# Seven-product pairs at two places of a feed-forward stage, their blocks loaded from another queue

## The reference

```python
def swiglu(x, w_in, w_out):
    gate, up = jnp.split(x @ w_in, 2, axis=-1)
    return (jax.nn.silu(gate) * up) @ w_out

# first block, i = 0, 1
x = x + 0.5 * swiglu(rms_norm(x, ffn1_norm_g[i]), ffn1_w_in[i], ffn1_w_out[i])   # ffn0, ffn2
x = x + concat(mixer_heads, memory_heads) @ w_out
x = x + 0.5 * swiglu(rms_norm(x, ffn2_norm_g[i]), ffn2_w_in[i], ffn2_w_out[i])   # ffn1, ffn3
# second block
h = h + hybrid_mixer(rmsnorm(h, norm_mix_w), ...)
h = h + (silu(n @ w_gate) * (n @ w_up)) @ w_down      # n = rmsnorm(h, norm_ffn_w): ffn4
return rmsnorm(h, final_norm_w)
```

## Time and profile before

| what | us |
|---|---|
| median of 3 runs | 1527.47 (1527.09 to 1528.89) |
| the profiled execution | 1527.58 |
| its span in the trace | 1525.9 |
| PE busy | 1515.7 |
| DVE busy | 1110.0 |
| ACT busy | 867.3 |
| POOL busy | 263.8 |

### The profile page before, as it was taken

How to read it: one execution, slowest core, us unless ns; L and a number is a source line. 1 busy time by engine, 2 the same in 40 slices (tenths; PEclk the granted TensorE clock), 3 DMA queues, 4 the chain that set the end, 5 groups by cost and what they waited for, 6 DMA issues and landing times.

```text
span 1525.9 us, 19569 instructions
## 1 busy us (share of the span) xinstructions
PE 1515.7 (99%) x7714; PEld 1281.9 (84%) x7714; DVE 1110.0 (73%) x1211; ACT 867.3 (57%) x1087; POOL 263.8 (17%) x216
## 2 busy tenths in 40 slices
PE   9999999999999999999999999999999999999998
PEld 7888888888888888888888888899988888888886
DVE  6687766556787568776776788599998568667875
ACT  7545554646455554556776455476887344454554
POOL 0222200001132122220001232100571000012220
PEclk9999999999999999999999999999999999999999
DMA  7997656446976699765416975666554665579762
GB/s 253 308 262 222 188 173 200 138 166 217 276 219 195 182 289 259 217 188 179 151 56 213 305 226 185 207 190 203 180 182 145 215 193 188 174 219 302 211 185 101
DMA packets 274307, 311.40 MB, mean 204 GB/s; under 512 B 64272, under 2 KB 233512, under 8 KB 274216
## 3 DMA queue, kind: packets, MB, share of 16 engines
q1 hardware_dynamic: 273112, 308.84, 65.4%
q10 hardware_dynamic: 1104, 1.31, 0.3%
HBM read 295.92 MB, written 1.09 MB: 195 GB/s over the span
## 4 chain that ended last, share of the span: by engine, by line
PE 94%; issue 2%; DVE 2%; ACT 1%; POOL 1%; DMA 1%; ACTq 0%; DVEq 0%; POOLq 0%
PE ps L2371 24%; PE ps L2375 24%; PE ps L2372 24%; PE ps L2413 3%; PE ps L2587 2%; PE ps L2588 2%; PE ps L2586 2%; PE ps L2361 2%; PE ps L2363 2%; PE ps L2362 2%; PE ps L2414 1%; PE ps L2429 1%; PE ps L2542 1%; DMA scr<-in_mem_dram 1%; PE ps L2693 0%
## 5 line engine op out<-in xcount | busy, mean ns | idle before, releaser
L1411 DVE TENSOR_TENSOR w_lo<-w_raw,w_hi 128x2048 fp32r<-128x2048 f32 x250 | 592.0, 2372 | 175.4 <-ACT w_hi L793 175.1
L793 ACT ACTIVATE w_hi<-w_raw 128x2048 fp32r<-128x2048 f32 x250 | 477.1, 1912 | 229.0 <-PE ps L2375 210.0
L2371 PE MATMUL ps<-w_hi,xg 128*128 128x512 f32 (+1 forms) x960 | 375.0, 391 | 0.0
L2375 PE MATMUL ps<-w_hi,xg 128*128 128x512 f32 (+1 forms) x960 | 372.1, 388 | 0.0
L2372 PE MATMUL ps<-w_lo,xg 128*128 128x512 f32 (+1 forms) x960 | 372.0, 387 | 0.0
L2371 PE MATMUL ps<-w_hi,y_hi 128*128 128x512 f32 x666 | 261.6, 393 | 0.5 <-DVE w_lo L1418 0.2
L2375 PE MATMUL ps<-w_hi,y_lo 128*128 128x512 f32 x666 | 259.1, 389 | 0.0
L2372 PE MATMUL ps<-w_lo,y_hi 128*128 128x512 f32 x666 | 258.9, 389 | 0.0
L761 POOL COPY scr<-scr 128x512 uint16<-128x512 uint16 x100 | 112.8, 1144 | 778.9 <-DVE scr L1526 778.9
L2371 PEld LDWEIGHTS ps<-w_hi,xg 128*128 128x128 f32 x960 | 180.3, 188 | 37.2 <-issue 0.7
L2375 PEld LDWEIGHTS ps<-w_hi,xg 128*128 128x128 f32 x960 | 180.2, 188 | 37.0
(11 more groups left out here) (409 smaller groups left out, 1864.1 us busy)
## 6 DMA issues: line engine op xcount, KB each, us to landing
w_raw<-in_ffn_w_in_dram SPq DMA_DIRECT2D x168, 512.0 KB, 4.9
w_raw<-in_ffn_w_out_dram SPq DMA_DIRECT2D x88, 512.0 KB, 4.8
w_raw<-in_w_in_dram SPq DMA_DIRECT2D x82, 512.0 KB, 4.5
w_raw<-in_a_w_in_dram SPq DMA_DIRECT2D x28, 512.0 KB, 4.6
w_raw<-in_w_down_dram SPq DMA_DIRECT2D x22, 512.0 KB, 4.5
w_raw<-in_w_gate_dram SPq DMA_DIRECT2D x21, 512.0 KB, 4.0
w_raw<-in_w_up_dram SPq DMA_DIRECT2D x21, 512.0 KB, 5.0
y_raw<-in_ffn_w_in_dram SPq DMA_DIRECT2D x16, 512.0 KB, 5.4
```

The lines of the kernel that those rows point to most:

```text
L793: act.activation(w_hi[:, u % RING, :], w_raw[:, u % RING, :], ACT.Copy).then_inc(w_rounded, 1)
L1411: dve.tensor_tensor(w_lo[:, s, :], w_raw[:, s, :], w_hi[:, s, :].bitcast(F32), ALU.subtract).then_inc(w_split, 1)
L2371: pe.matmul(dst, xh, hi, start=start, stop=False, skip_group_check=True)
L2375: return pe.matmul(dst, xl, hi, start=False, stop=stop, skip_group_check=True)
```

## The change

`PAIRS_OF` gives the pieces at which a pair begins, for each stage: 8 in ffn0 and ffn1, 4 and 8 in ffn2, ffn3 and ffn4, where before it was 7 in all five. Places of units come from `ffn_places`. SP no longer loads blocks. POOL does, at places between its cuts and joins; for a stage's second pair each block waits for the product of the first pair that reads the same buffer. The T and S work of DVE and ACT moves to the two or three steps ahead of the first pair, and that of a second pair to the end of the first and to step 7. The S sums and their parts are made once a stage and serve both pairs. A pair at 8 takes in the last piece, with its transposition on PE.

```diff
-PAIR = 7
-
-
-def gate_at(i, half):
-
-    if i < PAIR + 2:
-        return half if i == 0 else 3 * PAIR + 1 if i == PAIR + 1 else 3 * i - 1 + half
-    return 3 * i - (3 if i == PAIR + 2 else 2) + half
...
+PAIRS_OF = ((8,), (8,), (4, 8), (4, 8), (4, 8))
+
+def ffn_places(pairs):
+    order, i = [("G", 0, 0), ("G", 0, 1)], 1
+    while i < NI:
+        if i in pairs:
+            order += [("G", i, 0), ("G", i, 1), ("G", i + 1, 1), ("D", i - 1), ("G", i + 2, 0), ("G", i + 2, 1), ("D", i), ("D", i + 1)]
+            i += 3
+        else:
+            order += [("G", i, 0), ("G", i, 1), ("D", i - 1)]
+            i += 1
+    return {step: k for k, step in enumerate(order + [("D", NI - 1)])}
+PLACES = tuple(ffn_places(pairs) for pairs in PAIRS_OF)
...
@@ SP, ffn(f)
-                def block(k, half):
-                    j, part = half, gu_src(f, *((0, PAIR), (0, PAIR + 1), (1, PAIR + 1), (1, PAIR))[k])[half]
-                    dst = t_raw[k].rearrange("p (k c) -> p k c", k=4)[:, :, 256 * j:256 * j + 256]
-                    sp.dma_start(dst, part).then_inc(t_landed[k], 16)
...
-                    if i == 1:
-                        sp.wait_ge(w_used, u + 1)
-                    if i < 5:
-                        block(i - 1, 0)
...
-                    if i < 5:
-                        block(i - 1, 1)
+                def pair(p):
+                    gate_up(1, p)
+                    gate_up(1, p + 1)
+                    down(p - 1)
+                    turn_back(p - 1)
+                    gate_up(0, p + 2)
+                    gate_up(1, p + 2)
+                    down(p)
+                    down(p + 1)
+                    turn_back(p)
+                    if p + 3 < NI:
+                        gate_up(0, p + 3)
+                    else:
+                        down(NI - 1)
+                    turn_back(p + 1)
...
@@ POOL, ffn(f)
+                def block(p, k):
+                    half, i = ((0, p), (0, p + 1), (1, p + 1), (1, p))[k]
+                    if p == pairs[0]:
+                        pool.wait_ge(w_used, u + 1)
+                    else:
+                        pool.wait_ge(pe_done, pe_.at(f"M{(5, 7, 6, 4)[k]} {f} {pairs[0]}"))
+                    for j in range(2):
+                        dst = t_raw[k].rearrange("p (k c) -> p k c", k=4)[:, :, 256 * j:256 * j + 256]
+                        pool.dma_start(dst, gu_src(f, half, i)[j]).then_inc(t_landed[k], 16)
+
+                def blocks(i):
+                    if i + 5 == pairs[0]:
+                        block(i + 5, 0)
+                    if i + 4 == pairs[0]:
+                        block(i + 4, 1)
+                        block(i + 4, 2)
+                    if i + 3 == pairs[0]:
+                        block(i + 3, 3)
+                    if i + 5 in pairs[1:]:
+                        for k in (0, 2, 1):
+                            block(i + 5, k)
+                    if i + 3 in pairs[1:]:
+                        block(i + 3, 3)
+
+                blocks(-1)
                 cut(0)
                 join(0)
+                blocks(0)
                 for i in range(1, NI - 1):
                     cut(i)
                     pool.wait_ge(ffn_hl, NI * nth[f] + i)
                     join(i)
+                    blocks(i)
...
@@ ACT, step(i)
                     round_(v + 2)
                     hidden_high(i - 1, (i - 1) % 2)
-                    if i == 4:
-                        t_high(T1, f"T1 {f}")
-                    if i == 5:
-                        s_high()
+                    if i + 1 == pairs[0]:
+                        t_high(i + 1, T2, "T2")
+                    if i + 1 in pairs[1:]:
+                        t_high(i + 1, T1, "T1")
                     round_(v + 3)
+                    if i + 2 == pairs[0]:
+                        s_high()
                     for tt in range(2):
                         silu(i, tt)
-                    if i == 5:
-                        t_high(T2, f"T2 {f}")
+                    if i + 1 in pairs[1:]:
+                        t_high(i + 1, T2, "T2")
                     round_(v + 4)
+                    if i + 2 == pairs[0]:
+                        t_high(i + 2, T1, "T1")
...
@@ DVE, step(i)
                     split(v + 2)
                     hidden_low(i - 1, (i - 1) % 2)
-                    if i == 3:
-                        t_sum(T1, T3, T1, "T1")
-                    if i == 4:
-                        t_sum(T3, T2, T3, "T3")
-                    if i == 5:
-                        t_sum(T4, T4, T2, "T4")
-                    if i == 6:
-                        t_low(T2)
+                    if i + 2 == pairs[0]:
+                        t_sum(i + 2, T1, T3, T1, "T1")
+                    if i + 1 == pairs[0]:
+                        t_sum(i + 1, T4, T4, T2, "T4", "T2")
+                        s_lows((0, 1))
+                    if i + 1 in pairs[1:]:
+                        t_sum(i + 1, T4, T4, T2, "T4", "T2")
                     split(v + 3)
                     for tt in range(2):
                         product(i, tt)
-                    if i == 2:
+                    if i + 3 == pairs[0]:
                         x_sums()
-                    if i == 3:
-                        s_sums()
-                    if i == 4:
-                        t_sum(T2, T2, T1, "T2")
-                    if i == 5:
-                        t_low(T1)
-                    if i == 6:
-                        s_low_()
+                    if i + 2 == pairs[0]:
+                        t_sum(i + 2, T3, T2, T3, "T3", "T1")
+                    if i + 1 in pairs:
+                        t_low(i + 1, T1)
+                        t_low(i + 1, T2)
                     split(v + 4)
+                    if i + 3 == pairs[0]:
+                        s_sums()
+                    if i + 2 == pairs[0]:
+                        t_sum(i + 2, T2, T2, T1, "T2", "T3")
...
@@ DVE, pair(p)
                     split(n + 2)
-                    t_low(T3)
-                    t_low(T4)
+                    if p == pairs[0]:
+                        s_lows((3, 2))
+                    t_low(p, T3)
+                    t_low(p, T4)
...
                     split(n + 8)
+                    if p + 4 in pairs:
+                        t_sum(p + 4, T1, T3, T1, "T1")
+                        t_sum(p + 4, T3, T2, T3, "T3", "T1")
+                    if p + 2 == NI - 1:
+                        hidden_low(p + 2, p % 2, tiles(ps[:, 6, :]))
                     split(n + 9)
+                    if p + 4 in pairs:
+                        t_sum(p + 4, T2, T2, T1, "T2", "T3")
...
@@ PE, and alike on DVE, ACT and SP
+                while i < NI:
+                    if i in pairs:
+                        pair(i)
+                        i += 3
+                    else:
+                        step(i)
+                        i += 1
```

More of the change, by code:

```diff
@@ L106, in plan_units @@
     add("w_o", "dddd")
-    add("ffn4", ffn)
+    add("ffn4", ffn[4])
     return first, opens
@@ L2636, in ffn, with step @@
+                def step(i):
                     gates(i, taken(i - 1))
```

296 lines of the change are left out of this document (146 added, 150 removed).

## The result

| | median, us | range | runs |
|---|---|---|---|
| before | 1527.64 | 1526.33 to 1528.89 | 6 |
| after | 1536.91 | 1530.33 to 1542.2 | 6 |
| after, timed once more beside its repairs | 1534.15 | 1530.17 to 1535.05 | 5 |

The ratio after to before is 1.0060, 95% interval [1.0034, 1.0086]; in the second timing 1.0037 [1.0024, 1.0051], against a before of 1528.08 us. So the changed kernel is slower, by 6 to 9 us, where I forecast 5 us faster. Its runs scatter by 12 us, those of before by 2.6 us. The profiled execution is one of the short ones (1530.33 us), so what it shows is the lower part of the loss. Its granted clock was 0.999; the five longer runs of the first timing had 0.996 to 0.997.

The account below looks back on a forecast made before the run. PE was taken as the bound, so only fewer matmuls help: a span of 1525.9 - 8.16 + 3 x 1.1 = 1521.0 us, forecast 1522.6 us against 1527.58 us profiled. The range was 1519.0 to 1533.0 us.

Parts of the forecast that it names:

- What bounds the kernel, and the saving: PE is busy 1515.7 of 1525.9 us, so only fewer matmuls help; three added pairs take 8.16 us off.
- DVE ahead of the pair at 4: Ffn2 to ffn4, steps 1 to 3: DVE's preparation nearly fills its 53.4 us; cost 1.1 us a stage.
- Its signs: PE waits for w_lo or a DVE T low, ffn2 to ffn4, about 3 us in all; DVE over 15 us busy in step 3.
- Rival two: In steps 1 to 3 DVE becomes the bound: 3.3 us a stage, 1529.2 us, with full stretch 1535.8 us; chance 0.24.
- GpSimd's queue: Block issues by GpSimd between its cuts and joins take 1.2 us each and stay hidden in its idle time.
- Rival three: Slow GpSimd issues stall PE at down 1; 2.5 us each equals the saving, 3.3 us gives 1536.7 us; chance 0.16.
- DMA: 1 MB more ahead of or beside step 1's transposing transfer is 3.0 us; late by 0.1 or 1.6 us, nothing added.
- the deficit above: DVE's shortfall ahead of the pair at 4: 0.9 us a stage, taken as 1.1 us, bounds 0 and 5.5 us.
- The margins themselves: Step 1's hidden low part is done before PE wants it: by 2.9 us in ffn4, 1.4 us in ffn3.
- Rival four: Transfers crowd: step 1's transposing transfer or ring loads of steps 1 and 2 come late, some 4 us, 1526.6 us; chance 0.09.

Follow-up runs that it names:

- its repairs: Block 1 ahead of the first cut and U3 copied ahead of the rounding of unit n+5, in ffn2 to ffn4 alone, against the changed kernel: 1528.78 us.
- small ring transfers: The changed kernel with the ring transfers of ffn2, ffn3 and ffn4 cut to 64 columns of one row tile each: 1520.93 us.
- The runs at 4, 5 and 6: The changed kernel with one pair a stage, in ffn2 to ffn4 at step 4, 5 or 6: 1534.24, 1528.5 and 1527.73 us.
- the pair at 8: The changed kernel with one pair a stage, at step 8 in all five stages: 1527.36 us.
- small ring transfers in the first steps: One pair at 4 in ffn2 to ffn4, gate/up ring transfers of steps 1 to 3 and down ones of 0 and 1 cut small: 1529.54 us.

## Why the prediction was wrong

- **What bounds the kernel, and the saving.** Right. 36 matmuls are gone, and with small ring transfers 6.8 us of the 8.16 us appear (1527.74 to 1520.93).
- **DVE ahead of the pair at 4.** Its signs came, its reason was wrong. I took 3.3 us in three stages. In each of them TensorE's weight loads wait once for a split, a T low and a T high, 0.2 to 0.7 us each, 4.7 us in all, and DVE is busy for all of step 3. But where the ring's bytes are small no wait for a T low is left, 1.0 us for T highs stays, and all ungained time there is 1.6 us. DVE's own work just fits; the late hidden low part pushes it out. Rival two falls: DVE by itself isn't the bound.
- **GpSimd's queue.** Right that it is hidden: the issues behind join 0 end at 551.7 in ffn2, and the cut starts 2.4 us later. An issue takes 0.75 us against my 1.2. Rival three falls with it, far from its 2.5 us.
- **DMA. This is the step that failed**: "I add nothing to the deficit above". I had the place (the transposing transfer of step 1) and priced the added 1 MB at 3.0 us by its bytes. The join waited 8.22 us in ffn2, 5.0 us more than the 3.18 us of one step later, and 6.70 and 7.32 us in ffn3 and ffn4. And I let the lateness vanish into DVE's deficit ("DVE catches up by the same time"), where nothing vanished: DVE had no gap left in which to catch up. The runs at 4, 5 and 6 put 6.9, 1.1 and 0.4 us on the place alone (against the pair at 8; the 0.4 is within the noise), and small ring transfers in the first steps take back 4.7 us of the 6.9. The margins themselves were larger than I reckoned: in ffn3, where I had 1.4 us, a join 3.5 us later stalled TensorE not at all in step 1.
- **The term that wasn't in the sum at all**: the second pair's three blocks stand inside the first pair and delay the ring unit n + 5, with U3 behind it on ScalarE. I had looked there only for GpSimd's issues and found them hidden. Taking U3 ahead removes the wait for C21 (4.5 us). By medians it gains 3.9 us against the repeat and 6.7 us against the first timing, which were on other chips.
- **Rival four**, crowded transfers, was the mechanism, with 4 us and a chance of 0.09, and its sign came: cut 1 on time and a wait for the transfer over 7 us in two of three stages. What hangs on transfers measures 1534.15 - 1520.93 = 13.2 us to 1536.91 - 1520.93 = 16.0 us, the second place included, of which rival four says nothing.

My prediction quoted the Trainium skill's page DMA: Bandwidth & Descriptors, section "Issuing engines are not separate DMA queues", that all queues share the same 16 engines. The run with block 2 behind join 1 and U3 first agrees: the transposing transfer of step 1, on SP's queue, was issued at 557.89 us in ffn2 (557.31 in the changed kernel), had 1 MB less beside it on GpSimd's queue, and the join waited 4.85 us instead of 8.22. The run with the blocks on ScalarE's queue can't tell, since its waits come from ScalarE's time for the issues. I had read that rule as 3.0 us paid "somewhere" and then left it out of the sum.

Open: how the longer runs of the changed kernel come to their 4 to 12 us more than the profiled one. A mean clock of 0.996 against 0.999 is some 0.003 x 1534 = 4.6 us of it; where those stretches lie no profile caught. Open is why a small transfer is slowed by 5.0 us where the added bytes are worth 3.0 us. Also open is the 2.2 us that stay at the pair at 4 with small transfers ahead of it. Two pairs a stage with the first at 5 or 6 were not tried: this code asks for a step between the pairs to prepare the second.

## What to carry to other kernels

Before adding bytes to a stretch, list every small latency-bound transfer in it and ask what is queued behind each: here a wait of 3.2 us for a transfer became one of 8.2 us beside 2 MB, and bytes over bandwidth said 3.0 us in all. (Latency-bound means that its time is mostly not that of its bytes.) Then measure the room of the chain that the transfer belongs to. The same pair cost 6.9 us at step 4, 1.1 us at 5 and nothing measurable at 6 and 8; at 6 the transfers were as late as at 4, but the chain had 14.5 us, not 9.8 us, and VectorE had gaps. The DMA share didn't tell the places apart: it was 1.09 in both. On an in-order engine, put the instruction that waits for a DMA behind the copy that others need, not ahead of it.

## What the hardware showed that I had not expected

- A DMA of 512 KB is issued by GpSimd in 748 ns in the median and at most 892 ns in the changed kernel, beside 378 to 1506 ns on SP.
- GpSimd's queue moved 33.56 MB in 9216 packets, 3.6 KB each, where SP's had 284.72 MB in 248824, 1.14 KB each. On ScalarE's queue the same blocks (34.87 MB with its few others) are 34896 packets of 1.0 KB. Whether the size of the packets matters to the transfers beside them no run here tells.
- Single waits of TensorE of 4.45 and 3.44 us were followed by a granted clock of 0.79 and 0.85 over 8 us. One of 2.98 us was not, nor was any of up to 1.5 us in the profile of the changed kernel.
